# A gated delta rule whose keys stay unscaled: lengths from the diagonal of K times K, folded into per-token columns

## The reference, cut to what matters

```python
q, k, v = jnp.split(jax.nn.silu(conv(qkv)), ...)
q = l2norm(q) * GDN_DK ** -0.5          # per token and head
k = l2norm(k)
...
k_beta, v_beta = k * beta[..., None], v * beta[..., None]
l_strict = where(strict, einsum('bnthd,bnshd->bnhts', k_beta, k) * decay, 0.0)
t_inv = triangular_solve(eye + l_strict, eye)
u = einsum(t_inv, v_beta)
w = einsum(t_inv, k_beta * exp(g_cum))
att = where(incl, einsum(q, k) * decay, 0.0)
k_end = k * exp(g_cum[:, :, -1:] - g_cum)
# scan over chunks:
v_new = u_n - w_n @ s
o_n = (q * exp(g_cum)) @ s + att_n @ v_new
s = s * chunk_decay + k_end^T @ v_new
```

## Time and profile before

| | us |
|---|---|
| runs (median of 3) | 2183.26 (2180.09 to 2183.82) |
| profiled execution, its own time | 2180.62 |
| its span in the trace | 2178.7 |
| TensorE busy | 2109.8 (97%) |
| VectorE busy | 927.1 (43%) |
| ScalarE busy | 841.6 (39%) |
| GpSimd busy | 294.7 (14%) |

### The profile page before, as it was taken

The page is one execution under the profiler, slowest core; times in us unless marked ns, Lnnn a source line. Parts: engine busy times, 40 slices in busy tenths (PEclk is TensorE's granted clock), DMA queues, the critical chain, the costliest instruction groups (busy, mean ns, idle before and its releaser), DMA issues. The chain is left out here.

```text
span 2178.7 us, 31299 instructions
## 1 busy us (share of the span) xinstructions
PE 2109.8 (97%) x10890; PEld 1439.6 (66%) x10890; DVE 927.1 (43%) x2293; ACT 841.6 (39%) x2203; POOL 294.7 (14%) x623
## 2 busy tenths in 40 slices
PE   8999999999989999999999999999989979999998
PEld 5667576656556886555674446776676668976687
DVE  3023554857563235443231111246677653343321
ACT  1223354645443234444231112246556443245420
POOL 1000006153350000000000000000632641000000
PEclk9999999999999999999999999999999999999999
DMA  8326303221311022111122332231422312332333
GB/s 271 105 73 195 118 22 109 65 68 43 100 40 49 26 88 79 60 50 44 63 77 78 116 99 101 77 100 41 134 79 74 97 55 78 108 100 85 112 129 122
DMA packets 192443, 192.31 MB, mean 88 GB/s; under 512 B 28943, under 2 KB 186467, under 8 KB 191779
## 3 DMA queue, kind: packets, MB, share of 16 engines
q1 hardware_dynamic: 186048, 171.08, 25.4%
q0 software_dynamic: 4672, 18.89, 2.8%
q10 hardware_dynamic: 1571, 0.34, 0.1%
HBM read 180.78 MB, written 9.50 MB: 87 GB/s over the span
## 5 line engine op out<-in xcount | busy, mean ns | idle before, releaser
L1153 PE MATMUL bank<-hT,ring 128*128 128x512 f32 (+2 forms) x1856 | 715.1, 533 | 5.6 <-ACT hT L1557 3.6
L1153 PEld LDWEIGHTS bank<-hT,ring 128*128 128x128 f32 (+1 forms) x1856 | 331.7, 189 | 257.1 <-issue 239.1
L1153 PE MATMUL bank<-ring,hT 128*128 128x256 f32 (+2 forms) x2112 | 449.8, 368 | 0.0
L1153 PE MATMUL bank<-WORK 128*128 128x128 f32 (+6 forms) x3056 | 392.0, 286 | 37.3 <-DVE O L2202 13.3
L1153 PEld LDWEIGHTS bank<-ring,hT 128*128 128x128 f32 x2112 | 380.4, 190 | 62.4 <-issue 17.2
L1153 PEld LDWEIGHTS bank<-WORK 128*128 128x128 f32 (+4 forms) x3056 | 320.5, 170 | 144.9 <-issue 123.3
L1153 PE MATMUL bank<-yT,ring 128*128 128x512 f32 (+1 forms) x768 | 270.2, 489 | 0.0
L1153 PEld LDWEIGHTS bank<-yT,ring 128*128 128x128 f32 x768 | 139.2, 191 | 78.7 <-issue 69.7
L2126 DVE SCALAR_TENSOR_TENSOR WORK<-WORK,CW 128x512 f32<-128x512 f32 (+1 forms) x192 | 142.1, 740 | 2.2
L1512 ACT ACTIVATE E<-bank 128x512 f32<-128x512 f32 (+1 forms) x84 | 45.0, 536 | 207.4 <-PE bank L1153 198.2
L1116 POOL TENSOR_TENSOR WORK<-WORK 128x126 f32<-128x126 f32 (+22 forms) x248 | 107.3, 432 | 19.4
(11 more groups left out here) (215 smaller groups left out, 2009.6 us busy)
## 6 DMA issues: line engine op xcount, KB each, us to landing
ring<-in_w_in_dram SPq DMA_DIRECT2D x92, 1024.0 KB, 5.3
ring<-in_w_branch_dram SPq DMA_DIRECT2D x24, 1024.0 KB, 5.1
ring<-in_ada_w_dram SPq DMA_DIRECT2D x18, 1024.0 KB, 7.1
ring<-in_w_out_dram SPq DMA_DIRECT2D x8, 1024.0 KB, 5.1
WORK<-in_ada_w_dram SPq DMA_DIRECT2D x6, 1024.0 KB, 12.6
ring<-in_mla_q_up_dram SPq DMA_DIRECT2D x8, 576.0 KB, 4.1
xs<-yT POOLq DMA_DIRECT2D x2, 2048.0 KB, 7.5
WORK<-LD POOLq DMA_DIRECT2D x16, 256.0 KB, 3.4
```

Of the source, the lines that this page charges most:

```text
L1153: return nc.tensor.matmul(o, a, b, start=start, stop=stop, skip_group_check=True)
```

## The change

- Keys are no longer scaled. `dnq` and `dn` remain for the q tiles alone. The head's key products are of unscaled keys; VectorE multiplies their 128x256 block by the identity and sums (two new instructions in each `d2`) for the squared lengths, ScalarE takes Ln and Exp of eight columns (`rsqrt` in the last `dd`), and `KN8` holds one over the length for each token and head.
- In the last `dt` of a group seven small VectorE instructions make beta over length and beta over length squared (`KB`) and exp(g) over length (`EGK`, used by `sk` in place of `EGC`). SyncE writes `KB` to `BD` once in a group: 128 partitions x 16 x 8 bytes. GpSimd loads it (two DMAs, behind the two of `LD`).
- `dv` multiplies the inverted blocks by the length or by 1 (a product instead of a copy, and a reciprocal in front); `dx` and `dx6` multiply by `KN8` where they copied.
- The four transposes of beta, ScalarE's copy of them and the sixteen small DMAs of the old `BD` go.
- `AHEAD` has new numbers for 15 or so kinds; the group of `dqkv` items that stands before a head ends one item earlier. `sk` waits on VectorE for the `sa` before it and `su` for `sq`, since the list now lets them pass.
- Two semaphores become one (`s_spill`); nothing else of this part changes the waits.

```diff
-AHEAD = {('yT', 1, 0): 0, 'gw': 4, 'ga': 1, 'dnq': 1, 'yT': -1, 'cv': 6, 'ms': 1, 'mkv': 6, 'muk': -6, 'dx6': 3, 'dqkv': 5, 'd1': -1, 'muq': 2, 'dya': 2, 'vdn': -1, 'gv': 4, 'ab': 4, 'go': -4, 'dn': -3, 'mo': -8, 'vdsil2': 0, 'abT': -3, 'sq': -3, 'nx': 3, 'dy6': 3, 'dv': 1, 'dyb': 2, 'mod': 6, 'gatt': -6, 'gx': -4, 'z2': -4, 'sk': -1, 'dw2': -5, 'modT': -2, 'dw': 1, 'd3': 1, 'gb': -2, 'vz': 4, 'lr': -3, 'mqT': 3, 'vgate': -4, 'gqk': -1, 'dsilu': -2, 'norm': -2, 'vdsilu': -1, 'dg': -12, 'ge': -1, 'dgp': -2, 'out': 1}
+AHEAD = {('yT', 1, 0): 0, 'gw': 4, 'ga': 1, 'yT': 2, 'cv': 2, 'ms': 1, 'mkv': 6, 'muk': -2, 'dx6': 3, 'd1': -1, 'muq': 5, 'dya': 2, 'vdn': 3, 'gv': 4, 'ab': 3, 'go': -4, 'mo': -8, 'abT': 3, 'sq': -3, 'nx': 3, 'dy6': 3, 'dv': 1, 'dyb': 2, 'mod': 6, 'gatt': -6, 'gx': -4, 'z2': 4, 'sk': 2, 'dw2': -5, 'modT': -2, 'dw': 1, 'd3': 1, 'gb': -2, 'vz': 4, 'lr': -3, 'mqT': 3, 'vgate': -4, 'gqk': -1, 'dsilu': 2, 'norm': -2, 'dg': 0, 'ge': -1, 'dgp': 10, 'out': 1, 'dn': -3, 'su': 1}
...
                 tail = [("v", "dsilu") + v, ("dsil2",) + v, ("v", "dsil2") + v]
-                if v[2] < 4:
+                if v[2] < 2:
                     tail += [("dnq",) + v, ("dn",) + v, ("v", "dn") + v]
...
-                n = rest.index(("v", "dn", l, g + 1, 3)) + 1
+                n = rest.index(("v", "dsil2", l, g + 1, 3)) + 1
...
                     if rounds(l, g):
                         sp.wait_ge(s_lblk, 64 * rounds(l, g))
+                    if tt == TT - 1:
+                        sp.wait_ge(s_kbeta, rounds(l, g) + 1)
+                        sp.dma_start(BD[0, :].rearrange("(s p e) -> p s e", p=P, e=2),
+                                     KB[:, :, :, :].rearrange("p t u e -> p (t u) e")).then_inc(s_beta, 16)
+                    sp.wait_ge(*done(u, "dve"))
...
                         pool.dma_start(SLA[rows, :], systems(LD)).then_inc(s_lblk, 16)
-                        pool.dma_start(SLB[rows, :], BD[l, g].rearrange("t u (b i) -> (t u b) i", i=BASE)).then_inc(s_lblk, 16)
+                    pool.wait_ge(s_beta, 16 * (n + 1))
+                    for odd in range(2):
+                        rows = slice(odd * q, (odd + 1) * q)
+                        pool.dma_start(SLB[rows, :, :], BD[0, :].rearrange("(q i e) -> q i e", i=BASE, e=2)).then_inc(s_lblk, 16)
...
-                    mm(ps[:, 64:128], ONES[:, :], GG[:, :, :])
-                    for tt in range(TT):
-                        ins = tr(psum(it, 1)[0:16, tt * P:(tt + 1) * P],
-                                 BETA[:, tt, :])
+                    ins = mm(ps[:, 64:128], ONES[:, :], GG[:, :, :])
...
-                            pe.wait_ge(*done(("dn", l, g, j), "dve"))
+                            pe.wait_ge(*done(("dsil2" if j >= 2 else "dn", l, g, j), "dve"))
...
                 elif k == "dd":
                     _, l, g, tt = it
+                    if tt == TT - 1:
+                        act.wait_ge(s_ksum, TT * (rounds(l, g) + 1))
+                        kn = KN8[:, :, 2 * g:2 * g + 2]
+                        rsqrt(kn, kn, 1.0).then_inc(s_knorm, 1)
...
                     _, l, g, tt = it
-                    dve.wait_ge(*done(("d1", l, g, tt), "act"))
...
+                    diag = LTP[:, g % 2, tt, :].rearrange("p (h n) -> p h n", h=2)
+                    ln(V_.tensor_tensor(diag, ps[:, 0:256].rearrange("p (h n) -> p h n", h=2), bc(ident, 1, [P, 2, P]), ALU.mult))
+                    V_.tensor_reduce(KN8[:, tt, 2 * g:2 * g + 2], diag, AX_X, ALU.add).then_inc(s_ksum, 1)
+                    dve.wait_ge(s_ksum, TT * rounds(l, g) + tt + 1)
+                    dve.wait_ge(*done(("d1", l, g, tt), "act"))
...
+                    if tt == TT - 1:
+                        dve.wait_ge(s_knorm, rounds(l, g) + 1)
...
+                        for r in range(2):
+                            of = slice(r * BH + 2 * g, r * BH + 2 * g + 2)
+                            ins = V_.tensor_tensor(KB[:, :, 2 * r:2 * r + 2, 1], BETA[:, :, of], kn, ALU.mult)
+                        ln(ins)
+                        for r in range(2):
+                            ins = V_.tensor_tensor(KB[:, :, 2 * r:2 * r + 2, 0], KB[:, :, 2 * r:2 * r + 2, 1], kn, ALU.mult)
+                        ln(ins)
+                        ins = V_.tensor_copy(KB[:, :, 2:4, 1], KB[:, :, 2:4, 0])
+                        ins.then_inc(s_kbeta, 1)
+                        for r in range(2):
+                            of = slice(r * BH + 2 * g, r * BH + 2 * g + 2)
+                            V_.tensor_tensor(EGK[:, g % 2, :, 2 * r:2 * r + 2], EGC[:, :, of], kn, ALU.mult)
                     dve.wait_ge(*done(("dd", l, g, tt), "act"))
...
+                    if ("sa", l, g, n - 1) in where:
+                        dve.wait_ge(*done(("sa", l, g, n - 1), "pe"))
...
+                        if ("sq", l, g, n) in where:
+                            dve.wait_ge(*done(("sq", l, g, n), "pe"))
```

More of the change, by code:

```diff
@@ L572, in hybrid_block @@
         XD = nc.dram_tensor("XD", (1, SYSTEMS * BLOCK_D), F32, kind="Internal").ap()
-        BD = nc.dram_tensor("BD", (DEPTH, 4, TT, 4, P), F32, kind="Internal").ap()
+        BD = nc.dram_tensor("BD", (1, TT * 4 * P * 2), F32, kind="Internal").ap()
         top = {}
@@ L734, in hybrid_block @@
         s_ha = stack.enter_context(nc.semaphore("input_shifted_by_act"))
-        s_beta = stack.enter_context(nc.semaphore("beta_rows_out"))
+        s_beta = stack.enter_context(nc.semaphore("key_betas_out"))
+        s_ksum = stack.enter_context(nc.semaphore("key_squares"))
+        s_knorm = stack.enter_context(nc.semaphore("key_norms"))
+        s_kbeta = stack.enter_context(nc.semaphore("key_betas"))
         s_lout = stack.enter_context(nc.semaphore("l_out"))
@@ L1026, in _ @@
             todo = [(where[last_use[replaced[u]]] if u in replaced else -1, 0, n, u) for n, u in enumerate(units)]
-            todo += [(where[it], 1, 0, it) for it in plan if it[0] in ("dg", "dt")]
+            todo += [(where[it], 1, 0, it) for it in plan if it[0] == "dt"]
             for at, (_, scratch, _, u) in enumerate(sorted(todo, key=lambda t: t[:3])):
@@ L1349, in _ @@
                     _, l, g, tt = it
-                    for j in (2, 3):
-                        pe.wait_ge(*done(("dn", l, g, j), "dve"))
-                    pe.wait_ge(*done(("dsil2", l, g, 5), "dve"))
+                    for j in range(2, 6):
+                        pe.wait_ge(*done(("dsil2", l, g, j), "dve"))
                     for j in range(4):
@@ L1705, in _ @@
                     nc.scalar.activation(EGC[:, :, :], ps[:, 0:64].rearrange("p (t n) -> p t n", t=4), ACT.Exp)
-                    nc.scalar.activation(DEC[:, :, :], ps[:, 64:128].rearrange("p (t n) -> p t n", t=4), ACT.Exp)
-                    nc.scalar.activation(BT, psum(it, 1)[0:16, :].rearrange("p (t n) -> p t n", t=TT), ACT.Copy).then_inc(
+                    nc.scalar.activation(DEC[:, :, :], ps[:, 64:128].rearrange("p (t n) -> p t n", t=4), ACT.Exp).then_inc(
                         signal(it, "act", "bt"), 1)
@@ L2189, in _ @@
                     _, l, g = it
+                    if g == 0:
+                        ln(V_.memset(KF[:, :, 0:2], 1.0))
+                    dve.wait_ge(s_knorm, rounds(l, g) + 1)
+                    ln(V_.reciprocal(KF[:, :, 2:4], KN8[:, :, 2 * g:2 * g + 2]))
                     if g:
@@ L2203, in _ @@
                 elif k == "dx":
-                    ins = V_.tensor_copy(PXA, ps[:, 0:256].rearrange("p (s n) -> p s n", s=TT))
+                    _, l, g = it
+                    dve.wait_ge(s_knorm, rounds(l, g) + 1)
+                    ins = V_.tensor_tensor(two_heads(PXA), ps[:, 0:256].rearrange("p (s h n) -> p s h n", s=TT, h=2),
+                                           bc(KN8[:, :, 2 * g:2 * g + 2], 3, [P, TT, 2, BASE]), ALU.mult)
                 elif k == "dya":
@@ L2209, in _ @@
                 elif k == "dx6":
[L2210 removed]
+                    _, l, g = it
+                    ins = V_.tensor_tensor(two_heads(PXB), ps[:, :].rearrange("p (s h n) -> p s h n", s=TT, h=2),
+                                           bc(KN8[:, :, 2 * g:2 * g + 2], 3, [P, TT, 2, CH]), ALU.mult)
                 elif k == "dy6":
```

59 lines of the change are left out of this document (28 added, 31 removed).

## The result

The changed kernel takes **2225.86 us** in the median (2224.25 to 2230.67); the kernel before, run beside it, takes 2181.74. The ratio is 1.0204, with a 95% interval of 1.0192 to 1.0217. The change is **slower by 44 us**, where 2178 had been forecast and 2192 was the end of the range. The profiled execution's span is 2222.4 us.

A forecast was written before the change was run, and what follows sets the result against it. TensorE, busy 2109.8 of 2178.7 us, was taken to bound the kernel, with VectorE's head or the solver's path bounding at some `dx`. Nine stretches summed to -4.9 us, giving 2178 from a median of 2183.3; range 2163 to 2192.

The forecast's parts named there:

- third rival: Store of betas: its 8-byte pieces bound the solver and the change is slower, 2199 us; chance 0.12.
- three rounds on the solver's path: In three rounds `dv` waits for the solver's last DMA, 4.40, 1.42 and 3.97 us in the kernel before.
- 1: Layer 0, up to `dx` of group 0: four `dn`, beta and waits go; -6.0 us.
- 2: Layer 0, to `dx` of group 1: two `dn` go, 0.5 comes back for busy VectorE; -1.2 us.
- 3: Layer 0, to `dx` of group 2: VectorE's head bounds, starts earlier but lasts 4.7 longer; +2.0 us.
- 4: Layer 0, to `dx` of group 3: longer solver's path just about covered, scan's order helps a little; -0.5 us.
- 5 and 6: Layer 1, up to `dx` of group 0: two `dn` and beta go, -2.2; then longer solver's path, +3.0 us.
- 7: Layer 1, to `dx` of group 1: two `dn`, one wait and 1.5 of scan waits go, 0.5 back; -3.7 us.
- 8: Layer 1, to `dx` of group 2: VectorE's head bounds, as in layer 0; +2.0 us.
- 9: Layer 1, to `dx` of group 3: solver's path, 2.2 less 0.5; +1.7 us.
- second rival: VectorE bounds the heads of groups 1 and 2 as well, +8 to 10 us, so 2187; chance 0.18.
- The likeliest case: Whole kernel: the forecast of 2178 us, with its spread of 2172 to 2185; chance 0.45.

The follow-up runs named there:

- e2_before_store: Kernel before plus, in each round, an unread store of 2048 pieces of 8 bytes ahead of the last two `LD` blocks; 2222.6 us, ratio 1.0188.
- f3_sizes: Kernel before plus an unread 16 KB store behind each round's last `LD` blocks, cut into pieces differently by round; 2185.6 us, ratio 1.0018.
- f1_turned_no_diag: Changed kernel with betas turned and stored in 128-byte pieces, without the diagonal's product and reduction (squared length constant, output wrong); 2164.2 us, ratio 0.9914.
- e1_turned: Changed kernel with key betas turned by one more VectorE transpose and stored in 128 pieces of 128 bytes; 2186.3 us, ratio 1.0024.
- f2_turned_old_order: Changed kernel with betas turned and stored in 128-byte pieces, ten changed numbers of `AHEAD` set back; 2189.3 us, ratio 1.0036.

## Why the prediction was wrong

**The 8-byte store: the third rival held, and both its chance and its price were too low.** The prediction named the sign that decides (a landing of 8 us or more); e2_before_store shows 7.0 to 8.8 us, f3_sizes 7.8 and 7.9. (The changed kernel's own landing is not recorded, and most of these lie just under the 8, though far above the 4 that the forecast allowed.) I took "1.5 us more until the last `LD` block has landed" inside bounds of 0.4 and 9.5; the time was some 5.5. I chose the lower end since I took `WORK<-XD`, 2048 pieces of 64 bytes in 4.2 us, for the nearest row. It was nearest by number, but 64 bytes is just the size from which a piece costs nothing here, and that is a load into SBUF, not a store to DRAM.

**Who waits for `LD`: a waiter was missed.** For the added DMA I named what stands behind it on SyncE's queue and priced the solver's path alone, so that even my third rival came to 21 us instead of 39.5. ScalarE's copy in the first `st` waits for the same semaphore, a line that the change doesn't touch; in the kernel before it never showed as a wait, as the blocks had landed. That is the wait that no row of before shows, and it took 19.7 us in ScalarE's row and 21 of the 28 us in the table. The weight load behind the store suffers too, 10.3 us to landing instead of 5.4, but nobody waited for it.

**What held.** The claim that the prediction staked most on, three rounds on the solver's path, is right: it is the same three in which `dv` sits idle, 9.77, 12.36 and 11.45 us. The waits at `dx` of group 2 are 9.7 and 8.6 us, where 8 to 10 were forecast. And the parts add up: with neither the 8-byte store nor the diagonal (f1_turned_no_diag) the kernel is 17.0 us below the one before; the diagonal's 22.1 and the store's 39.5 make 44.6 of it, for 44 measured.

**The rest of the sum, by e1_turned**, whose store has the cost that I had assumed. It should have come out at 2178 and takes 2186.3. Its stretches against the forecast, from the table of `dx`:

| stretch | forecast | measured |
|---|---|---|
| 1 | -6.0 | -6.9 |
| 2 | -1.2 | +1.3 |
| 3 | +2.0 | +2.3 |
| 4 | -0.5 | +2.2 |
| 5 and 6 | +0.8 | +1.2 |
| 7 | -3.7 | +2.1 |
| 8 | +2.0 | +7.0 |
| 9 | +1.7 | +2.0 |
| after the delta rule | 0 | -3.5 |

- Stretches 1, 3, 5 with 6, and 9 are right within 1 us: TensorE's work that goes, and the solver's path.
- In stretch 3 this is partly luck. The prediction says that the last key is ready 3.9 us before L2150 ended; by the earlier trace rows that is 4.6 (590.7 to 595.3), and 3.9 is to its start. With 4.6 the bracket is +1.4 to +2.4 instead of +2.1 to +3.1, and the reason given for taking +2.0 is about the other layer.
- Stretch 4 was 2.7 us worse than forecast. Between `dx` of group 2 and that of group 3 TensorE is busy for 49.1 us with 432 instructions, in the kernel before for 47.5 with 428; ahead of `dx` of group 2 it has 4 fewer (621 against 625). The new order has put more behind this `dx`, and the sum had priced no such move. Stretch 3 gained by it.
- Stretches 2 and 7 are the step of the second rival. I let 0.5 come back where 4.8 us of VectorE's work arrive; f1_turned_no_diag puts 1.5 and 2.1 on the diagonal there. It was right that twelve items of projection take up most of a late head.
- In stretch 7 the gain of 1.5 from `sk` and `su` moved ahead did not come: TensorE's waits in the scans of groups 0 and 1 of layer 1 are 1.3 to 2.7 us each in e1_turned, against 0.9 and less in the earlier trace rows. 
- Stretch 8 is where the sum failed by most. I had copied layer 0's +2.0 ("as in 3"); the diagonal alone costs 7.4 there, against 4.2 in stretch 3. The 3.0 between them is the clock, which the prediction has no term for: 6.6 us of this stretch's work ran at half clock. The waits cost the same in both layers.
- Of the 3.5 us at the end, 2.37 are a wait for the transposes of `yT` in the kernel before, which the new order has removed (with `yT` set back, in f2_turned_old_order, it is there again). I had given that no row. The rest is open.

**The likeliest case** was therefore wrong by 8 us in its own terms and by 48 with the store. Of the views that I named as a test, the late landing of the store showed it. The sign of the second rival is there too, but small: at `dx` of groups 0 and 1 the new waits are 1.26 us (layer 0, group 0) and 0.26 (layer 1, group 1) of the 49.2.

## What to carry to other kernels

Before a DMA is put into a queue, ask for every engine that waits on the semaphore of what stands behind it, also on lines that the change doesn't touch, and price a store by size and place of its pieces: one 32-column transpose that makes them 128 bytes was worth 39.5 us here. Where an engine's stretch bounds (here VectorE's head), count its added instructions in each round that hangs on it, and look for one instruction that does the work of two before moving the work to an engine that is full.

## What the runs showed of the hardware

- A DMA store of 16 KB to DRAM from 128 partitions landed 1.5 us after its issue in 128-byte pieces, 1.6 in 64-byte pieces, 2.5 in 32, 3.5 in 16, 4.4 in 8-byte pieces at 64 or 512 bytes from each other, and 7.8 to 7.9 in 8-byte pieces side by side, while in e2_before_store the DMA engines were busy for only about 1.7 us of 7.2.
- What was queued behind such a store on SyncE landed about when it did: 32 KB blocks took 6.5 us instead of 1.6, and one 1 MB load 10.3 instead of the median of 5.4.
- VectorE's product with accumulator over 128x128 from PSUM took 0.28 us and its read-out 0.08, with the next product started 0.21 us after the first: two heads in 0.53 us, against 0.90 for a product and a reduction over 128x256 with a link between them.
- A product of a 128x128 tile with one column costs TensorE 0.127 us for each of its two instructions, about as much as eight transposes' 0.11 each.
- Behind some of its waits (2.23 us in e1_turned, 5.44 in e2_before_store) TensorE's granted clock stood at 0.50 for a while, 6.8 us in the first, and its work took twice as long: four 512-column matmuls in 3.62 us instead of 1.7.
